# Transposing the softmax probabilities: eight TensorE transposes per tile, or a trip through DRAM with VectorE block transposes

## The reference

```python
for l in range(2):
    h = rms_norm(x, norm_mix[l])
    proj = h @ w_in[l]                     # (2048, 2048): q, k, v, pool, retention q, k, v, gate
    y_a = sliding_window_sink_attention(q_a, k_a, v_a, ...)
    y_b = multiscale_pool(u_b, ...)
    y_c = retention(q_c, k_c, v_c, g_c, pos)
    x = x + concat(y_a, y_b, y_c) @ w_out[l]
    x = x + moe_ffn(rms_norm(x, norm_ffn[l]), router_w, router_b, w_gate[l], w_up[l], w_down[l])

def sliding_window_sink_attention(...):    # 8 heads of 64, 2 kv heads, chunks of 64
    sc = einsum('bnqhgd,bnkhd->bnhgqk', qb, kb) * 64 ** -0.5     # 64 queries x 128 keys
    p = softmax(concat([sc, sink], -1))[..., :-1]
    o = einsum('bnhgqk,bnkhd->bnqhgd', p, vb)
```

## Time and profile before

| | |
|---|---|
| median of 3 runs | 3073.78 us |
| span of the profiled execution | 3111.4 us |
| PE busy | 3053.7 us, 98% of the span |
| DVE busy | 1395.4 us, 45% |
| ACT busy | 614.5 us, 20% |
| granted TensorE clock (core's mean) | 0.998 |
| part one of layer 0 / layer 1 | ends at about 780 us / runs from about 1560 to 2352 us |

### The profile page before, as it was taken

One profiled execution on the slowest core, in us unless ns is written; L12 is line 12 of the kernel. 1 busy time (PEld: TensorE's weight loads), 2 busy tenths in 40 slices (PEclk: granted clock), 3 DMA queues, 4 the chain that ended last, 5 costly groups with the idle time before them and its releaser, 6 DMA issues.

```text
span 3111.4 us, 54691 instructions
## 1 busy us (share of the span) xinstructions
PE 3053.7 (98%) x18148; PEld 2179.5 (70%) x18148; DVE 1395.4 (45%) x4000; ACT 614.5 (20%) x1922; POOL 1059.8 (34%) x1250
## 2 busy tenths in 40 slices
PE   8999999999999999999999999999999999999998
PEld 4555555555799999888755555555558999998886
DVE  5576677666322222211155676676663222222111
ACT  1322322322111111101123223222221111111101
POOL 1232133223255555423212232232233555553322
PEclk9999999999999999999999999999999999999999
DMA  8756655653698899999865656657546889999996
GB/s 307 262 192 232 241 206 216 249 194 139 228 301 295 296 317 323 339 355 348 324 247 192 210 211 251 214 196 251 186 156 232 290 298 314 318 314 346 345 356 215
DMA packets 248184, 817.11 MB, mean 263 GB/s; under 512 B 68016, under 2 KB 121264, under 8 KB 188720
## 3 DMA queue, kind: packets, MB, share of 16 engines
q1 hardware_dynamic: 200912, 734.26, 63.9%
q0 software_dynamic: 46112, 77.70, 10.7%
q10 hardware_dynamic: 864, 1.47, 0.2%
HBM read 718.87 MB, written 95.56 MB: 262 GB/s over the span
## 4 chain that ended last, share of the span: by engine, by line
PE 94%; DVE 2%; DMA 1%; issue 1%; SPq 1%; ACT 0%; another core or an unknown queue 0%; DVEq 0%; POOL 0%; ACTq 0%; POOLq 0%
PE bank L2089 32%; PE bank L1792 19%; PE bank L1857 14%; PE bank L2129 9%; PE bank L2119 7%; PE bank L1763 4%; PE bank L1713 2%; PE bank L1943 1%; PE bank L1984 1%; PE bank L2018 1%; DMA arena<-in_x 1%; PE bank L1868 1%; PE bank L1718 1%; PE bank L1952 0%; DVE arena L1231 0%
## 5 line engine op out<-in xcount | busy, mean ns | idle before, releaser
L2089 PE MATMUL bank<-arena,wts 128*128 128x128 f32 (+7 forms) x8192 | 1007.5, 283 | 21.5 <-issue 19.9
L2089 PEld LDWEIGHTS bank<-arena,wts 128*128 128x128 f32 x8192 | 989.9, 191 | 49.2 <-issue 46.3
L1792 PE MATMUL bank<-wts 128*128 128x512 f32 x1056 | 469.5, 596 | 0.0
L1857 PE MATMUL bank<-wts,arena 128*128 128x512 f32 x1024 | 453.9, 595 | 1.2 <-ACT arena L1059 1.2
L1688 DVE TENSOR_TENSOR arena<-arena,bank 128x128 f32<-128x128 f32 (+6 forms) x64 | 19.1, 299 | 945.8 <-ACT arena L1121 945.8
L828 POOL DMA_INDIRECT arena<-hrows,arena x288 | 292.5, 1016 | 167.7 <-issue 152.6
L1792 PEld LDWEIGHTS bank<-wts 128*128 128x128 f32 x1056 | 195.0, 190 | 219.7 <-issue 218.1
L1857 PEld LDWEIGHTS bank<-wts,arena 128*128 128x128 f32 x1024 | 189.4, 190 | 216.1 <-issue 214.1
L724 POOL TENSOR_TENSOR arena<-arena 128x256 f32<-128x256 f32 x32 | 25.5, 796 | 858.0 <-DVEq L1424 858.0
L853 POOL DMA_INDIRECT out<-arena x176 | 275.1, 1563 | 56.9 <-issue 53.7
L2129 PE MATMUL bank<-arena,wts 128*128 128x135 f32 (+6 forms) x2176 | 280.0, 289 | 0.0
(11 more groups left out here) (267 smaller groups left out, 3145.9 us busy)
## 6 DMA issues: line engine op xcount, KB each, us to landing
wts<-in_w_gate SPq DMA_DIRECT2D x128, 1024.0 KB
wts<-in_w_up SPq DMA_DIRECT2D x128, 1024.0 KB
wts<-in_w_down SPq DMA_DIRECT2D x128, 1024.0 KB
wts<-wt SPq DMA_DIRECT2D x96, 1024.0 KB, 6.0
wts<-in_w_in SPq DMA_DIRECT2D x88, 1024.0 KB, 7.4
hrows<-arena SPq DMA_DIRECT2D x36, 512.0 KB, 5.7
out<-arena SPq DMA_DIRECT2D x36, 512.0 KB, 3.3
wt<-arena SPq DMA_DIRECT2D x16, 1024.0 KB, 4.0
```

The source lines that it names most:

```text
L1792: i = mm(bIP[j in (1, 3, 6)][:, :], own[:, d], ring[k % SLOTS][:, d], start=(d == 0 and j in (0, 1, 3)), stop=(d == 3), skip_group_check=True)
L1857: i = mm(bIP[k][:, :], dT[o][:, d - 4] if d in (4, 5) else mixT[:, d], wout[:, d, 512 * k:512 * k + 512], start=(n == 0), stop=(n == DC - 1))
L2089: return mm(gu_at(f, k, w), lhs, xT[:, d, 0:w], start=start, stop=(d == DC - 1), skip_group_check=True)
```

## The change

In steps 1 to 15 of each layer (30 times in all), `pr` has another order of columns, `(quarter, head, 32)` in place of `(head, 128)`. ScalarE stores it to a DRAM scratch of 512 KB (`probs_rows`, two of them) as soon as `probs_ready` is raised, waits for the store behind the router's exponentials, and issues four loads of 128 KB each that put the quarters on the partitions. VectorE waits for the four loads behind `z`, and does one block transpose of 128x1024 into `prT`. TensorE's eight transposes and ScalarE's two copies go. Step 16 keeps the old way.

```diff
+    probs_rows = [nc.dram_tensor(f"probs_rows{b}", (P, D), F32).ap() for b in range(2)]
@@ scalar engine
-                                a(pr[:, k, g], (bC, bD)[k][:, g * P:(g + 1) * P], ACT.Exp, bias=stat[:, 16 + n:17 + n],
-                                  scale=1.0, accum_out=stat[:, 24 + n:25 + n])
+                                src = (bC, bD)[k][:, g * P:(g + 1) * P]
+                                a(head_probs(s, n), src if s == TILES else src.rearrange("p (q c) -> p q c", q=4), ACT.Exp,
+                                  bias=stat[:, 16 + n:17 + n], scale=1.0, accum_out=stat[:, 24 + n:25 + n])
...
+                    if back and s < TILES:
+                        wait_alone(e, probs_ready, t0)
+                        e.dma_start(probs_rows[o], pr_flat).then_inc(probs_stored, 16)
...
+                    if back and s < TILES:
+                        wait_alone(e, probs_stored, (l * (TILES - 1) + s) * 16)
+                        for k in range(4):
+                            e.dma_start(pr_flat[32 * k:32 * k + 32, :].rearrange("p (g c) -> p g c", g=4),
+                                        probs_rows[o][:, PIECE * k:PIECE * k + PIECE].rearrange("(g s) c -> s g c", g=4)).then_inc(probs_in, 16)
...
-                        e.wait_ge(pe_pT, t0)
-                        for k in range(2):
-                            a(prT[:, k].rearrange("p g n -> p (g n)"), (bC, bD)[k][:, :], ACT.Copy)
-                        e.drain().then_inc(pT_ready, 1)
                         if s == TILES:
+                            e.wait_ge(pe_pT, l + 1)
+                            for k in range(2):
+                                a(prT[:, k].rearrange("p g n -> p (g n)"), (bC, bD)[k][:, :], ACT.Copy)
+                            e.drain().then_inc(pT_ready, 1)
@@ vector engine
+                            by_quarter = pr_flat.rearrange("p (q n c) -> p q n c", q=4, n=8)
+                            v.tensor_tensor(by_quarter, by_quarter, bc(stat[:, 24:32].unsqueeze(1).unsqueeze(3), [P, 4, 8, 32]),
+                                            ALU.mult).then_inc(probs_ready, 1)
...
                         e.drain().then_inc(z_ready, 1)
+                    if back and s < TILES:
+                        e.wait_ge(probs_in, (l * (TILES - 1) + s) * 64)
+                        v.transpose(prT.rearrange("p a g (k s) -> p k (a g) s", k=4), pr_flat)
+                        e.drain().then_inc(pT_ready, 1)
@@ tensor engine
-                    if back:
+                    if s == TILES:
                         e.wait_ge(probs_ready, t0)
-                        if front:
-                            e.wait_ge(uT_ready, t0 + 1)
                         for a in range(2):
                             for g in range(4):
                                 i = tr((bC, bD)[a][:, g * P:(g + 1) * P], pr[:, a, g])
```

More of the change, by code:

```diff
@@ L260, in program @@
         probs_at = used["mix"]
-        pr = part("mix", 1024).rearrange("p (a g n) -> p a g n", a=2, g=4)
+        pr_flat = part("mix", 1024)
+        pr = pr_flat.rearrange("p (a g n) -> p a g n", a=2, g=4)
         prT = part("mix", 1024).rearrange("p (a g n) -> p a g n", a=2, g=4)
@@ L324, in program @@
         vw_ready = sem("vw_ready")
+        probs_stored, probs_in = sem("probs_stored"), sem("probs_in")
         pe_oproj, x_new = sem("pe_oproj"), sem("x_new")
@@ L430, in by_d, with head_probs @@
             return tile.rearrange("p (d n) -> p d n", n=P)
+        def head_probs(s, n):
+            if s == TILES:
+                return pr_flat[:, P * n:P * n + P]
+            return pr_flat.rearrange("p (q n c) -> p n q c", q=4, n=8)[:, n]
         def slot_full(l, k):
@@ L1395, in step @@
                         e.drain()
-                        v.tensor_tensor(pr.rearrange("p a g n -> p (a g) n"), pr.rearrange("p a g n -> p (a g) n"),
-                                        bc(stat[:, 24:32].unsqueeze(2), [P, 8, P]), ALU.mult).then_inc(probs_ready, 1)
+                        if s == TILES:
+                            v.tensor_tensor(pr.rearrange("p a g n -> p (a g) n"), pr.rearrange("p a g n -> p (a g) n"),
+                                            bc(stat[:, 24:32].unsqueeze(2), [P, 8, P]), ALU.mult).then_inc(probs_ready, 1)
+                        else:
+                            by_quarter = pr_flat.rearrange("p (q n c) -> p q n c", q=4, n=8)
+                            v.tensor_tensor(by_quarter, by_quarter, bc(stat[:, 24:32].unsqueeze(1).unsqueeze(3), [P, 4, 8, 32]),
+                                            ALU.mult).then_inc(probs_ready, 1)
                     if front and back and s < LATE:
```

## The result

The changed kernel takes **3351.4 us** (median of 4 runs, 3344.6 to 3361.4) against 3073.3 for the kernel before (median of 4, 3072.9 to 3074.6): a ratio of **1.0903**, with an interval of [1.089, 1.0916]. It is slower, as forecast, but by 278 us instead of 45, and outside the range. The profiled execution has a span of 3349.1 us.

A forecast was written before the change was run, and what follows sets the result against it. TensorE, 94% of the chain, was taken to bound the kernel; factored steps +31.8, steps 14 and 15 +10.4 and step 1 +3.0 us made +45.2 on 3073.8, so 3119 us, range 3086 to 3172.

The forecast's parts named there:

- slack: Time between VectorE's `finish_columns(s, 2)` ending and TensorE's need of it: 1.52 us in step 6, 0.60 in step 5.
- hit hardest: Expected sign in the profile after: steps 14 and 15 suffer most; predicted losses 3.5 and 1.7 us.
- All landed: T + 0.1 + 5.7 + 4.3 = T + 10.1: Factored steps: issue delay 0.1, store 5.7 and four loads 4.3 us, so the data is back at T + 10.1.
- T: End of VectorE's multiplication by the reciprocal sums; predicted times count from it (332.95 in step 6, 286.76 in step 5).
- The 5.7: Predicted time in us of ScalarE's 512 KB store, from a row for the same bytes stored amid weight loads.
- The argument against it: Against the 8.5 us store: 2.4 MB pass in 6 us, so what waits at T should be through.
- The 3.0 for the loads: Predicted us from issue to landing of the last load, which starts 1.3 after the first: 4.3 in all.
- What TensorE sees of it: Factored steps: the wait at the projection's second half swallows the 0.88 us saved; mean loss 1.33 us, +31.8 over 24.
- d: Predicted lateness of everything on VectorE behind the block transpose: 2.21 us in step 6, 2.56 in step 5.
- rival 4: VectorE's router instructions fall behind GpSimd's rotary work, shortening its chain by up to 1.1 us per step: 3068; chance 0.04.
- Rival 3: Contention makes the store take 8.5 us, landing at T + 12.9: sum +121, 3195 us; chance 0.18.
- Rival 2: The trip fits: store 2.6 us, loads landing at T + 9.15: sum +15.6, 3089 us; chance 0.22.

The follow-up runs named there:

- experiment 1: Changed kernel without the store and loads, block transpose right behind `z` on untransposed blocks; total 3842.5 us not comparable, factored-step period 46.34 us against 46.18 before.
- experiment 6: Kernel before plus the 512 KB store and a load of half of it into a spare tile, TensorE and VectorE not waiting: 3075.3 us, 1.0002.
- experiment 2: Changed kernel with SP waiting for the trip's loads before issuing the weight block behind product 3 of a factored step: 3133.3 us, 1.0192.
- experiment 3: Changed kernel with ring blocks carrying a quarter of their bytes, rest not loaded; only the mixing part is read: period 46.15 us.
- Experiment 4: Changed kernel with 24 idle products on constants on TensorE ahead of PV, filling part of its wait: 3328.4 us, 1.0827.
- experiment 7: Kernel of experiment 6 with 1 KB store pieces (3110.7 us) or SP issuing the store (3115.5); changed kernel with 1 KB store pieces, one load: 1.0632.

## Why the prediction was wrong

**Right.** TensorE bounds the kernel, and only its waits count. VectorE's `finish_columns(s, 2)` has no slack to give: without a trip, 0.85 of the 0.88 us are lost in each factored step on average (experiment 1). The multiplication in runs of 32 columns costs nothing (1.22 us in the rows of both; an exponential takes 0.38 us in the mean in both). The block transpose takes 1.245 us. Step 14 has the longest wait of all, 13.26 us in layer 0, and had been put at 3.5 us of loss. Of step 15 "hit hardest" was wrong: its 3.31 and 3.49 us are the two shortest waits. The ring isn't starved, and the traffic costs nothing that can be measured (experiment 6). The expert part is unchanged.

**The step that failed first: "All landed: T + 0.1 + 5.7 + 4.3 = T + 10.1".** Both transfer times were too small. In step 6 the store took 9.2 us (issued 380.68, landed about 389.9) in place of 5.7, and the loads 6.8 (from 389.94 to about 396.8) in place of 4.3. All had landed at T + 16.2. The 5.7 was the median of a row over the whole span; in the factored steps of the kernel before, the same row has a median of 6.7 us, and the row of ScalarE's own queue, 8.5, which I had set aside, was nearer to what came. The argument against it was that 2.4 MB pass in 6 us, so that what waits at T should be through by then. It takes the bytes that wait at T for all there are; here SP issues two more blocks between 378.86 and 382.63, around T (380.58), and those share the engines too. The 3.0 for the loads was from a time with no ring block under way. The next blocks were, at 388.15:

```profile
375.37 0.33 SPq L551 DMA_DIRECT2D wts<-wt  x1
378.86 3.77 SPq L551 DMA_DIRECT2D wts<-in_w_in  x2
388.15 3.76 SPq L551 DMA_DIRECT2D wts<-wt  x2
```

Experiments 2 and 3 show the cause: with the blocks held back or cut, the loads take 2.9 us in both, and the store 4.6 and 2.7. With the blocks held back the median trip of a factored step, from the store's issue to the last landing, is 9.2 us in place of 16.5. In layer 0's step 13, whose wait of 11.26 us is the second longest there, SP issues two blocks at 770.28, right ahead of the loads at 771.47, which is the same pattern.

**The second step: "What TensorE sees of it".** With d at 8.7 instead of 2.2 us the wait lands on PV, not on the last columns. From there it doesn't add up again at the columns, because VectorE's chain up to the end of `finish_columns(s, 2)` became 1.9 us shorter in step 6: from the transpose's end at 398.05 to 405.61 it is 7.6 us, against 9.5 from `z`'s end before. Over the 24 factored steps it is 8.0 us in the mean against 10.1. The router's comparison takes 0.28 us where it took 0.82, and GpSimd's rotary work, which starts with `z`, is over by then (at 394.82). In experiment 1, where nothing is late, the chain is 9.9 us long. That is the mechanism of rival 4, seen with a landing so late that it gains nothing. The Trainium skill's "SBUF — State Buffer", section "Who interferes with whom", says that VectorE and GpSimd share a port pair under an exclusive lock, and that an instruction of VectorE with two inputs in SBUF contends for it with a GpSimd instruction that reads SBUF. The 0.82 and 0.28 us agree with it.

**The term that was not there: the clock.** I read each wait as its own length. After 29 of the 30 waits (3.49 to 13.26 us) TensorE came back at the 1.2 GHz level. After the one of 3.31 us, in layer 0's step 15, PV took 1.15 us and the clock fell right behind it:

```profile
878.53 8.41 PE L1884 MATMUL bank<-wts,arena 128*128 128x512 f32 x16
```
```profile
878.20:880.00 1.80, 1.80 (x4) 1.00 (x5) 1.60 (x4) 0.94 (x2) 1.48 (x3) 0.50 0.00 0
```

From PV to the rank sums the thirty steps needed 2.2 us more than before in the mean, 66 us in all. Experiment 4 took part of it back, 2.4 us in its step 9.

**The rivals.** Rival 3, contention, had the mechanism and nearly the store's time (8.5 against 8.2), but kept the idle loads and left the clock out: 3195, where 3351 was measured. Rival 2, the trip that fits, had T + 9.15; experiment 2's factored steps come near it once the ring is held back, with a trip of 9.2 us, though the store takes 4.6 of it and not 2.6. The Trainium skill's "DMA: Bandwidth & Descriptors", section "Anatomy of one DMA", fits its formula to transfers that GpSimd issues, which the prediction doesn't say: this store is ScalarE's. Used all the same it gives an estimate of 3.2 us. Measured were 2.7 on engines with room (experiment 3) and 8.2 in the changed kernel, so for this store it was near on engines with room and far off on full ones. The same page's section "Queues, rings and completion order" has the engines take turns between the queues with work. I had read it as speaking for a quick store. A queue of its own gave no advantage, 8.1 against 7.7 us in the weights' queue (experiment 7), and nothing here shows the turns themselves.

What stays open: how the engines share out between the two queues packet by packet. The runs show only that the store's time hardly depends on its queue.

## What to carry to other kernels

A transfer is priced by what is in flight when it is issued and what is issued before it lands, in that stretch, not by its row over the whole span; a round trip through DRAM on a critical path needs a stretch that is kept free of bulk loads, and then it may cost little (1.0903 became 1.0192 by one wait on the weights' queue, and 0.9984 with the trip in the factored steps alone and the columns moved up). Before work is taken from the engine that bounds, look whether the engine that feeds it has slack: here 0.85 of 0.88 us turned into a wait until the feeding instruction was moved up as well. And a wait of TensorE is priced with the slower stretch behind it, here 0.9 to 3.0 us on top of waits of 3.3 to 13.3, and 1.6 and 1.7 on top of two waits of about 2.

## What the hardware showed beyond expectation

- The same 512 KB store takes 2.7 us in the median with small blocks, where a stretch around a store has a DMA share of 0.50, and 9.2 in step 6 of the changed kernel, at a share of 1.00 and 396 GB/s (medians of 8.1 to 8.2); a load of 128 KB 2.9 and 5.4. Full engines triple the latency of a store, though the kernel's throughput didn't suffer in experiment 6 (3075.3 against 3074.4 us).
- TensorE came back at a granted clock of 0.50 (1.2 GHz) after its long waits, and lost 2.2 us in the mean (2.49 in step 5) in work that takes 8.17 at the full clock. Waits of 1.99 and 2.26 us had the fall behind them too, while the other waits of the factored steps in that kernel, of up to 1.88 us, had not. Idle products on constants ahead of PV kept it at 1.00 (2.4 GHz) in nine of layer 0's fifteen steps.
- Moving VectorE's work behind GpSimd's shortened it by 1.9 us in step 6 and by 2.1 in the mean of the factored steps, without any change to its instructions.
